# Three-layer block on one core: the first layer entered by groups of 512 channels, its modulation as wide products with an accumulator and as whole columns

## What is computed

```
mod = jnp.dot(jax.nn.silu(c), w_ada) + b_ada          # c: one row of 2048, w_ada: 2048 x 6144
shift, scale, gate = jnp.split(mod, 3, axis=-1)
u = rms_norm(x, norm_w) * (1.0 + scale[:, None, :]) + shift[:, None, :]
proj = jnp.dot(u, w_in)                               # w_in: 2048 x 19064
```

## Time and profile before

| | us |
|---|---|
| median of 3 runs | 3603.05 (3601.96 to 3606.71) |
| the profiled execution, its own time | 3606.82 |
| its span in the profile | 3605.0 |
| TensorE busy | 3485.0 (97%) |
| VectorE busy | 2280.1 (63%) |
| ScalarE busy | 1689.4 (47%) |
| granted TensorE clock, mean | 0.977 |
| moved by DMA | 705.67 MB |

### The profile page before, as it was taken

One profiled execution on the slowest core, in us unless ns is written; L12 is line 12 of the kernel. 1 busy time (PEld: TensorE's weight loads), 2 busy tenths in 40 slices (PEclk: granted clock), 3 DMA queues, 4 the chain that ended last, 5 costly groups with the idle time before them and its releaser, 6 DMA issues. The chain is left out here.

```text
span 3605.0 us, 45068 instructions
## 1 busy us (share of the span) xinstructions
PE 3485.0 (97%) x18836; PEld 2997.6 (83%) x18836; DVE 2280.1 (63%) x2722; ACT 1689.4 (47%) x2076; POOL 31.1 (1%) x61
## 2 busy tenths in 40 slices
PE   7999999998999999999999999999999999999998
PEld 7779878877888887799888888888888789988887
DVE  7687666756677456677655576664566676554544
ACT  2354564454333344545644543433445775443333
POOL 0000000000000000000000000000000000000000
PEclk7899999999999999999999999999999999999999
DMA  9654455456667545444444367765555444455554
GB/s 374 231 203 158 152 199 198 175 185 231 257 253 287 200 181 196 163 161 146 162 144 149 124 223 254 256 258 193 187 187 181 167 166 141 153 211 193 191 186 153
DMA packets 99387, 705.67 MB, mean 196 GB/s; under 512 B 11680, under 2 KB 11696, under 8 KB 15600
## 3 DMA queue, kind: packets, MB, share of 16 engines
q1 hardware_dynamic: 93888, 675.38, 51.5%
q0 software_dynamic: 4864, 24.95, 2.0%
q10 hardware_dynamic: 432, 2.45, 0.2%
HBM read 696.45 MB, written 6.29 MB: 195 GB/s over the span
## 5 line engine op out<-in xcount | busy, mean ns | idle before, releaser
L1365 ACT ACTIVATE HH<-RAW 128x2048 fp32r<-128x2048 f32 x546 | 1045.2, 1914 | 1201.5 <-PE G L1107 905.1
L1701 DVE TENSOR_TENSOR LL<-RAW,HH 128x2048 fp32r<-128x2048 f32 x546 | 1248.0, 2287 | 337.2 <-ACT HH L1365 335.8
L1107 PE MATMUL G<-HH,UH 128*128 128x512 f32 x2560 | 1028.0, 402 | 33.2 <-DVE LL L1701 27.6
L1107 PE MATMUL G<-LL,UH 128*128 128x512 f32 x2560 | 1006.4, 393 | 0.0
L1107 PE MATMUL G<-HH,UL 128*128 128x512 f32 x2560 | 1006.0, 393 | 0.0
L1107 PE MATMUL G<-UH,HH 128*128 128x256 f32 x2080 | 605.0, 291 | 14.5 <-DVE LL L1701 8.4
L1107 PEld LDWEIGHTS G<-HH,UH 128*128 128x128 f32 x2560 | 485.9, 190 | 154.2 <-DVE LL L1701 37.4
L1107 PE MATMUL G<-UL,HH 128*128 128x256 f32 x2080 | 590.5, 284 | 0.0
L1107 PE MATMUL G<-UH,LL 128*128 128x256 f32 x2080 | 590.4, 284 | 0.0
L1107 PEld LDWEIGHTS G<-LL,UH 128*128 128x128 f32 x2560 | 485.6, 190 | 104.9
L1107 PEld LDWEIGHTS G<-HH,UL 128*128 128x128 f32 x2560 | 486.4, 190 | 102.2 <-issue 4.1
(11 more groups left out here) (327 smaller groups left out, 2506.9 us busy)
## 6 DMA issues: line engine op xcount, KB each, us to landing
RAW<-in_w_in_packed_dram SPq DMA_DIRECT2D x402, 1024.0 KB, 4.8
RAW<-in_w_ada_packed_dram SPq DMA_DIRECT2D x96, 1024.0 KB, 5.1
RAW<-in_w_out_packed_dram SPq DMA_DIRECT2D x48, 1024.0 KB, 4.8
RAW<-in_w_o_ssd_packed_dram SPq DMA_DIRECT2D x32, 1024.0 KB, 4.8
RAW<-in_w_o_fox_packed_dram SPq DMA_DIRECT2D x16, 1024.0 KB, 4.8
RAW<-in_w_o_dsa_packed_dram SPq DMA_DIRECT2D x16, 1024.0 KB, 5.2
RAW<-in_w_proj_a_packed_dram SPq DMA_DIRECT2D x16, 1024.0 KB, 4.8
RAW<-in_w_proj_b_packed_dram SPq DMA_DIRECT2D x16, 1024.0 KB, 4.8
```

Source lines behind the costliest of these rows:

```text
L1107: mm = pe.matmul(to, lt, rh, start=first, stop=end, skip_group_check=True)
L1365: a.activation(HH[g % NH][:, :n], RAW[ch["f"] % NR][:, :n], ACT.Copy).then_inc(*hi_done.up(g))
L1701: v.tensor_tensor(LL[f % NR][:, :n], RAW[f % NR][:, :n], HH[g % NH][:, :n].bitcast(F32), ALU.subtract).then_inc(*lo_done.up(g))
```

## The change

- Layer 0's shift and scale are no longer made for all channels first. `open` goes through four groups of 512 input channels. A group has 8 dots of 128 outputs each: 5 on VectorE (`dot_dve`: `w_ada` transposed, 128 outputs as partitions, 2048 wide, times a broadcast row `CB` of silu(c), summed by the instruction's accumulator into one column of `DOT`) and 3 on TensorE (`dot_pe`: 16 matmuls with one column that add up over all 2048 inputs). Each dot reads one chunk of 1,024 KB. There is no fold for them.
- Then `am` and `u` of this group alone, and the three blocks `IQ`, `IQ`+512 and `DK` each take their chunk of this group. These chunks are multiplied among the dots of the next group. The third block uses `BA`, `BC` as its banks.
- During the opening there are 8 buffers (`NR` + `NX`; the three more lie in memory of `YH`, `YL`). At its end the ring goes back to five, beginning with buffer 0. A fetch waits for the last reader of its buffer, whoever it was.
- `misc` follows the three blocks. The second layer's `w_ada` chunks are taken one for two product chunks instead of two for five until conv, and begin after the opening.
- ScalarE makes the squares of `x` before its first planned step; the rotary tables come in the slots of the opening's products.

```diff
@@ fetch
+        f = len(self.fetches)
+        buf = self.next_buf % (NR + NX if self.opening else NR)
+        self.next_buf += 1
+        self.fetches.append({"src": src, "at": (name, self.packed[name] - 1), "reader": reader, "buf": buf,
+                             "before": self.buf_user.get(buf)})
+        self.buf_user[buf] = f
+        return f
@@ new
+    def dot(self, kind, ct, engine):
+        c0 = (D if kind == "scale" else 0) + ct * P
+        src = ("w_ada_turned", 0, c0, P, [(0, D)]) if engine == "dve" else ("w_ada", 0, 0, D, [(c0, P)])
+        token = ("dot_" + engine, kind, ct)
+        self.dots[token[1:]] = self.fetch(src, token)
+        self.put(*token)
+
+    def open(self, blocks, between, enter):
+        for gi in range(4):
+            old = [b["chunks"][gi - 1] if gi else None for b in blocks]
+            dots = [("shift", 1, "pe"), ("scale", 0, "dve"), ("scale", 1, "dve"), ("shift", 2, "pe"), ("scale", 2, "dve"),
+                    ("scale", 3, "dve"), ("shift", 3, "pe"), ("shift", 0, "dve")]
+            for i, (kind, m, engine) in enumerate(dots):
+                if i == 7:
+                    new = blocks[0]["chunks"][gi]
+                    self.bring(new)
+                self.dot(kind, 4 * gi + m, engine)
+                if i in (2, 5) and gi:
+                    ch = old[1 + i // 5]
+                    self.bring(ch)
+                    self.put("lo", ch["g"])
+                if i in (0, 3) and gi:
+                    self.gemm(old[i // 3])
+                    self.slot()
+                if not gi:
+                    between(i)
+            enter(gi)
+            if gi < 3:
+                self.put("lo", new["g"])
+            if gi:
+                self.gemm(old[2])
+                self.slot()
+        self.opening, self.next_buf = False, 0
+        self.pend.append(blocks[0]["chunks"][3])
+        for b in blocks[1:]:
+            self.push(b["chunks"][3])
@@ work_order
-    o.ada_all()
-    while o.side.q:
-        o.slot()
...
+            *iq_b, dkv_b = [o.wblock(w, c0, heads(h), u_ready, kind="tm", begun=True, which=i)
+                            for i, (c0, h) in enumerate(firsts)]
+            o.open([*iq_b, dkv_b], first_x, enter_first)
+            o.ada["list"] += [(1, b, k) for b in range(8) for k in range(4)]
+            o.ada["every"] = (1, 2)
+            misc_b = o.block([one], misc(l), ("U", 0), u_ready, KT)
@@ TensorE
+        def dot(kind, ct):
+            f = o.dots[kind, ct]
+            to = (BD, BE)[ct // 4 % 2][:, ct % 4:ct % 4 + 1]
+            pe.wait_ge(*landed(f))
             pe.wait_ge(*c_silu.at())
+            if ct >= 8:
+                pe.wait_ge(*am.at(0, ct // 4 - 2))
+            for k in range(KT):
+                mm = pe.matmul(to, RAW[buf(f)][:, k * P:(k + 1) * P], CT1[:, k:k + 1], start=k == 0, stop=k == KT - 1)
+            mm.then_inc(*dot_pe.up(kind, ct))
@@ ScalarE, begin
+            a.dma_start(CB[:, :], A["c"][0].partition_broadcast(P)).then_inc(*ld_cb.up())
...
+            a.wait_ge(*ld_cb.at())
+            a.activation(early[:, 0:D], CB[:, :], ACT.Tanh, scale=0.5).then_inc(*cb_tanh.up())
+            for t in range(2):
+                a.wait_ge(*ld_x[t].at())
+                a.activation(xK[:, t, :], kv2[:, t, :], ACT.Square, accum_out=SSQ[:, t:t + 1]).then_inc(*x_sum.up(t))
@@ VectorE
+            v.wait_ge(*cb_tanh.at())
+            v.scalar_tensor_tensor(CB[:, :], early[:, 0:D], 1.0, CB[:, :], ALU.add, ALU.mult).then_inc(*cb_silu.up())
+
+        def dot(kind, ct):
+            f = o.dots[kind, ct]
+            c = (16 if kind == "scale" else 0) + ct
+            v.wait_ge(*landed(f))
+            v.wait_ge(*cb_silu.at())
+            v.scalar_tensor_tensor(RAW[buf(f)][:, :], RAW[buf(f)][:, :], 0.5, CB[:, :], ALU.mult, ALU.mult,
+                                   accum_out=DOT[:, c:c + 1]).then_inc(*dot_dve.up(kind, ct))
@@ VectorE, am of layer 0
+        def am_first(gi):
+            c = 4 * gi
+            pe_part = (BD, BE)[gi % 2]
...
+            v.wait_ge(*dot_dve.at("shift", c))
+            v.tensor_tensor(AM[:, c:c + 4], DOT[:, 16 + c:20 + c], MOD[:, 16 + c:20 + c], ALU.add).then_inc(*own.up())
+            v.tensor_tensor(SH[:, c:c + 1], DOT[:, c:c + 1], MOD[:, c:c + 1], ALU.add).then_inc(*own.up())
+            v.wait_ge(*own.last())
+            v.scalar_tensor_tensor(AM[:, c:c + 4], AM[:, c:c + 4], 1.0, PA[:, c:c + 4], ALU.add, ALU.mult).then_inc(*own.up())
+            v.wait_ge(*dot_pe.at("shift", c + 3))
+            v.wait_ge(*own.last())
+            v.tensor_tensor(SH[:, c + 1:c + 4], pe_part[:, 1:4], MOD[:, c + 1:c + 4], ALU.add).then_inc(*am.up(0, gi))
```

More of the change, by code:

```diff
@@ L115, in __init__ @@
         self.evac_before, self.side_before = {}, {}
-        self.user = [None, None]
-        self.ada = {"list": [], "i": 0, "job": None, "job2": None, "every": 0, "count": 0, "n": 0, "both": True,
-                    "next": 0, "got": []}
+        self.user, self.turns = [None, None, None], 0
+        self.ada = {"list": [], "i": 0, "job": None, "every": 0, "count": 0, "n": 0, "next": 0, "got": []}
         self.ada_info, self.folds = [], []
+        self.dots = {}
     def put(self, *token):
@@ L195, in gemm @@
                 self.slot()
-            b["free"] = user["free_by"] or user["end"] if user is not None else ("start",)
+            if user is None:
+                b["free"] = ("x_put", KT // 2 - 1) if b["set"] == 2 else ("start",)
+            else:
+                b["free"] = user["free_by"] or user["end"]
         self.put("gemm", ch["g"], 0)
@@ L238, in ada_fetch @@
         self.ada["next"] += 1
-        both = self.ada["both"] and kc == 3
         src = ("w_ada", l, kc * 512, 512, [(blk * 512, 512)])
-        f = self.fetch(src, ("ada_pe", i) if both else ("ada_acc", i, 3))
-        self.ada["got"].append(f)
+        self.ada["got"].append(self.fetch(src, ("ada_acc", i, 3)))
     def ada_chunk(self):
@@ L250, in ada_chunk @@
         n = a["n"]
[L251 to L257, removed]
+        self.ada_info.append({"l": l, "blk": blk, "kc": kc, "f": f, "n": n})
+        if kc == 0:
+            self.until(a["job"])
+        self.put("ada", i)
         if kc == 3:
-            self.folds.append({"l": l, "blk": blk, "both": a["both"], "i": i, "row": blk >= 8})
-            a["job2"] = a["job"]
+            self.folds.append({"l": l, "blk": blk, "i": i, "row": blk >= 8})
             a["job"] = self.evac.add(self.fold(n))
@@ L303, in side_ended, with first_x @@
         o.side_last = event
[L305 to L311, removed]
+    def first_x(i):
+        if i == 1:
+            put("x_norm", 0)
+            put("x_norm", 1)
+        if i == 3:
+            for c in range(KT // 2):
+                put("x_in", c)
     def rope(r):
@@ L597, in lru @@
         yield
-    o.ada["list"] = [(0, b, k) for b in range(8) for k in range(4)]
     put("start")
-    for gen in (first_x(), load_layer(0), rope(0), rope(1)):
+    for gen in (load_layer(0), rope(0), rope(1)):
         o.side.add(gen)
-    o.ada_all()
-    while o.side.q:
-        o.slot()
[L609 to L612, removed]
+    entered = []
     loaded = [None]
@@ L781, in hybrid_stack @@
     EPT = sb("EPT", [P, 1])
+    DOT = sb("DOT", [P, 32])
     over = []
@@ L1334, in lru_pe @@
             mm.then_inc(*lru_mm.up(ct))
-        todo = {"gemm": gemm, "start": begin, "ada_pe": ada_chunk, "fold": fold_pe, "x_in": x_in, "xn_pe": xn_pe,
+        todo = {"gemm": gemm, "start": begin, "dot_pe": dot, "fold": fold_pe, "x_in": x_in, "xn_pe": xn_pe,
                 "m_turn": m_turn, "hd_turn": hd_turn, "misc_pe": misc_mm,
```

171 lines of the change are left out of this document (88 added, 83 removed).

## The result

| | before | after |
|---|---|---|
| median of the runs beside each other, us | 3602.51 | 3628.61 (3627.31 to 3630.86) |
| the profiled execution, its own time, us | 3606.82 | 3630.86 |
| its span, us | 3605.0 | 3629.1 |

A forecast was written before the change was run, and what follows sets the result against it. TensorE's matmul issue bounds nearly all the span, transfers the opening. Overlapping 12 product chunks brings `DQ` from 194.0 to 178.5 us, 15.5 gained: span 3589.5, own time 3591.3, median 3588 us; range 3570 to 3608.

The forecast's parts named there:

- a pair: Opening: one product chunk (mean 6.7 us) with its column product on TensorE (3.7 us), 10.4 us together.
- half and half of cold starts: Opening: half the product chunks start at half clock (7.9 us each), the rest at full clock; mean chunk 6.7 us.
- Ring stall: Opening's end: reset to buffer 0 makes the next fetch wait for the previous chunk's matmuls; TensorE idle 9.3 us.
- the sum: Whole kernel: `misc` ends at 178.5 us against `DQ` at 194.0 before, 15.5 us gained, nothing changed behind it.
- (c): Opening: VectorE's wide products at half rate, 4.6 us each, about 14 us lost, 3602 us; chance 0.07.
- (a): Opening: full clock, transfers bound at 2.6 us a chunk, 28 us gained, 3575 us; chance 0.13.
- (d): Opening: clock stays at half throughout, `misc` ends at 244, 50 us lost, 3653 us; chance 0.10.
- (b): Opening: every product chunk starts at half clock, pairs of 11.6 us, 8 us more, 3596 us; chance 0.12.
- (f): Opening: no overlap as written, a fetch or VectorE wait holds the ring; no change, 3603 us; chance 0.02.
- (e): Behind the opening: side lane, 11 slots late, holds `FG`'s evacuation, gain comes back, about 3600 us; chance 0.04.
- the last part of the sum: Behind the opening: fewer second-layer `w_ada` chunks before conv, three later under the branches with free slots; costs nothing.
- The chance of "slower": Whole kernel: 0.10 that the change is slower, all from the clock staying at half through the opening, 3653 us.

The follow-up runs named there:

- e3: The changed kernel, with the ring going on at buffer 2 instead of 0 at the end of the opening; 3620.93 us, ratio 1.0043.
- e2: The kernel before, old opening, with the second layer's `w_ada` chunks at (1, 4) instead of (2, 5) until conv; 3633.52 us, ratio 1.008.
- e5: The changed kernel with the second layer's `w_ada` rate until conv set back from (1, 2) to (2, 5); 3615.59 us, ratio 1.0032.
- e11: The changed kernel at its rate (1, 2), `w_ada` groups fetched only after the previous fold, counter set back two chunks at layer 0's branches; 3585.85 us, ratio 0.9953.
- e9: The changed kernel with rate (2, 5) until conv and the `w_ada` counter set back by two chunks at layer 0's branches; 3592.7 us, ratio 0.9969.
- e8: The changed kernel with the ring going on at buffer 2 and `w_ada` chunks three for four until conv; 3616.27 us, ratio 1.0028.
- e6: The changed kernel with rate (2, 5) until conv and the ring going on at buffer 2; 3607.39 us, ratio 1.0006.

## Why the prediction was wrong, point by point

**Opening, right in its parts.** The first product came at 46.74 (45.7 predicted). The groups took 35.4, 32.5 and 32.9 us between the starts of their first chunks (32, 33 and 33 predicted), the last chunk of the first block ended at 154.9 instead of 150, since group 1 was 3.4 us longer and a pair took 11.2 and not 10.4 us: half and half of cold starts was a little too kind. Ring stall 9.0 (9.3 predicted), shown by e3. `misc` ended at 183.6 (178.5), 5.1 us late. Then came something that the sum lacks: four transposes (line 1251) and a wait of 2.2 us for line 1497, the copy that frees the bank of an earlier block, 2.8 us together. That makes 7.9 us: so 7.6 us were gained at `DQ` and not 15.5.

**Rivals.** (c) is refuted: `dot_dve` took 2.288 us for 2048 elements with its accumulator, plus 0.08 for reading it, the slope of the earlier trace rows and not twice that. The rule of the Trainium skill, "Vector Engine (DVE) Microarchitecture Reference", section 7, isn't borne out for this form here: with the accumulator the rate is that of the rows without. (a), the full clock, didn't come (0.81 from 80 to 140 us), nor did (d), the half clock throughout. The opening came out between the forecast and (b): pairs of 11.2 us (10.4 and 11.6), the first block's end at 154.9 (150 and 158). (f) didn't come: the first product started at 46.74. (e) named the right region and the wrong carrier: the loss isn't `FG` waiting for a late side lane, since e2 has it with the old opening.

**The step that failed** is the last part of the sum, "Four instead of seven chunks of the second layer's `w_ada` are taken before conv, three more later ...: nothing". I had counted the transfers and VectorE's work of these chunks, which indeed cost about 1 us (from `DQ` to chunk 23 after falls back by 1.9 us and e5, with the old rate, by 0.9), and not what a group's first chunk does to the queue: `until` on the fold of the group before. By the trace that step, which the sum has at nothing, cost 31 us from `DQ` to chunk 109, and by e11 against after 43 us can be had back. The chance of "slower" was 0.10 and stood wholly on the clock. That the change is slower by another mechanism was not among the rivals, although the line `self.until(a["job"])` is in the code of both kernels and the list of forced steps can be had from the plan before anything runs.

**What is shown and what isn't.** Shown: the rate alone makes the loss (e2); the place of the folds makes the four steps (e5 against e9); with the emptyings and the crowded gates removed the change gives about the predicted gain (e11: 17 us by the ratio and by the medians), which is partly luck, since only 7.6 us of it are there at `DQ`. Not undone one by one were the forced runs at 54, 92, 94 and 103, so how the 31 us divide between them is only read from the trace (those chunks took 12.3, 6.5, 15.9 and 5.1 us longer than before's, with several us given back between). How much of each is wait, half clock, or work that is only done earlier than before is not separated either.

## What to carry to other kernels

Where one list orders all engines and a step may say "empty the queue until X is done", a change of any rate or count moves these points for the rest of the kernel: list the forced runs before and after a change, by chunk, and price each by the chain of steps ahead of X. The number of forced steps alone tells little (e8). And subtract the starts of the same chunk in the two traces: a total of +26 us was a gain of 8 and a loss of 31 us, 300 to 700 us later, which neither the page's shares nor the total could have told. When an experiment that should bring the time back doesn't, the same subtraction shows whether the theory fell or a second cause took over.

## What the hardware showed that I had not expected

- After 9.02 us of idle time, or after 4.93 us of it and then one-column matmuls, the first matmul of the next product chunk took 0.77 to 0.79 us, that of half clock (163.90 and 879.38). After 2 to 3 us of waiting it went either way, with the wait the same to 0.01 us: 0.47 us in after and 0.77 in e6 ahead of the same chunk, and 0.47 (895.40, above) and 0.77 at two places of e5. So a forced step can cost a half-clock start of the next chunk on top of its wait, and by its length a wait of this size does not tell. In after, e6 and e5:

```profile
186.42 0.47 PE L1179 MATMUL G<-HH,UH 128*128 128x512 f32 x1 [2.20 <-ACT S L1497]
```

```profile
172.20 0.77 PE L1179 MATMUL G<-HH,UH 128*128 128x512 f32 x1 [2.20 <-ACT S L1497]
```

```profile
1037.34 0.77 PE L1179 MATMUL G<-HH,UH 128*128 128x512 f32 x1 [2.67 <-ACT WW L1578]
```

- The transfers of transposed `w_ada` in the opening took 12.4 us from issue to landing, against 4.8 for the product's over the whole run, though both are 1,024 KB. The page of after:

```profile
RAW<-in_w_in_packed_dram SPq DMA_DIRECT2D x402, 1024.0 KB, 4.8
...
RAW<-w_ada_turned_packed_dram SPq DMA_DIRECT2D x20, 1024.0 KB, 12.4
```

All twenty lie in the opening, where the eight buffers allow several to be under way together. The layout has little part in it: from 0 to 150 us the other chunks of 1,024 KB took nearly as long, 11.6 us for the ten of `w_in` and 9.4 for the twelve of `w_ada` as it was. The prediction had 4.8 for the opening too.

```profile
RAW<-in_w_ada_packed_dram SPq DMA_DIRECT2D x12, 1024.0 KB, 9.4
RAW<-in_w_in_packed_dram SPq DMA_DIRECT2D x10, 1024.0 KB, 11.6
```
